# Gate products of FFN tile pairs by seven block products in place of eight

## The reference, cut to what matters

```
for l in range(2):                       # first block
    mod = silu(c) @ w_ada[l] + b_ada[l]  # nine vectors of 1024
    x = x + 0.5 * g1 * swiglu(modulate(x, sh1, sc1), ffn1_gate[l], ffn1_up[l], ffn1_down[l])
    x = x + g2 * token_mix(modulate(x, sh2, sc2), ...)
    x = x + 0.5 * g3 * swiglu(modulate(x, sh3, sc3), ffn2_gate[l], ffn2_up[l], ffn2_down[l])
x = rms_norm(x) * final_norm
# second block
x = x + merged @ w_o
h2 = rms_norm_2(x, norm2_g)
x = x + square(relu(h2 @ w_up)) @ w_down

def modulate(x, shift, scale): return rms_norm(x) * (1 + scale) + shift
def swiglu(u, w_gate, w_up, w_down): return (silu(u @ w_gate) * (u @ w_up)) @ w_down
```

## Time and profile before

| | us |
|---|---|
| median of three runs | 3475.17 (3474.67 to 3475.22) |
| the profiled execution | 3478.61 |
| its span | 3476.8 |
| PE busy | 3429.5 (99%) |
| weight loads, DVE, ACT busy | 2745.0, 1755.9, 1194.8 |

### The profile page before, as it was taken

How to read it: one execution, slowest core, us unless ns; L and a number is a source line. 1 busy time by engine, 2 the same in 40 slices (tenths; PEclk the granted TensorE clock), 3 DMA queues, 4 the chain that set the end, 5 groups by cost and what they waited for, 6 DMA issues and landing times.

```text
span 3476.8 us, 40836 instructions
## 1 busy us (share of the span) xinstructions
PE 3429.5 (99%) x16684; PEld 2745.0 (79%) x16684; DVE 1755.9 (51%) x3020; ACT 1194.8 (34%) x2015; POOL 263.1 (8%) x220
## 2 busy tenths in 40 slices
PE   9999999999999999999999999999999999999999
PEld 7888786778888788887777888887778777878887
DVE  7666446565666733334655643334453555364433
ACT  3222236543222322223555332223322344233322
POOL 0000210002000200021100100013011000020000
PEclk9999999999999999999999999999999999999999
DMA  7565321123565533223210322322222223122332
GB/s 252 201 215 187 107 89 63 43 70 118 190 220 194 183 99 101 93 95 107 72 49 25 109 91 81 111 82 93 75 80 72 68 70 120 40 94 91 98 102 79
DMA packets 120361, 376.36 MB, mean 108 GB/s; under 512 B 13296, under 2 KB 28272, under 8 KB 120176
## 3 DMA queue, kind: packets, MB, share of 16 engines
q1 hardware_dynamic: 120176, 373.76, 32.7%
...
## 4 chain that ended last, share of the span: by engine, by line
PE 93%; DVE 4%; ACT 2%; issue 0%; DMA 0%; POOL 0%; SPq 0%; DVEq 0%; ACTq 0%; POOLq 0%
PE ps L449 27%; PE ps L451 26%; PE ps L450 26%; PE ps L671 2%; PE ps L694 2%; PE ps L566 2%; PE ps L483 1%; PE ps L484 1%; PE ps L485 1%; PE ps L499 1%; PE ps L492 1%; DVE s_wl L1481 1%; ACT s_wh L964 0%; PE ps L536 0%; PE ps L538 0%
## 5 line engine op out<-in xcount | busy, mean ns | idle before, releaser
L1481 DVE TENSOR_TENSOR s_wl<-s_raw,s_wh 128x1024 fp32r<-128x1024 f32 (+3 forms) x645 | 706.1, 1096 | 899.5 <-ACT s_wh L964 898.3
L449 PE MATMUL ps<-s_uh,s_wh 128*128 128x512 f32 x2824 | 1129.3, 400 | 12.4 <-DVE s_ul L1542 3.8
L451 PE MATMUL ps<-s_ul,s_wh 128*128 128x512 f32 x2824 | 1105.6, 392 | 0.5 <-issue 0.5
L450 PE MATMUL ps<-s_uh,s_wl 128*128 128x512 f32 x2824 | 1105.3, 391 | 0.0
L964 ACT ACTIVATE s_wh<-s_raw 128x1024 fp32r<-128x1024 f32 (+3 forms) x645 | 588.0, 913 | 731.0 <-PE ps L451 536.3
L449 PEld LDWEIGHTS ps<-s_uh,s_wh 128*128 128x128 f32 x2824 | 533.6, 189 | 156.2 <-issue 42.1
L451 PEld LDWEIGHTS ps<-s_ul,s_wh 128*128 128x128 f32 x2824 | 533.1, 189 | 114.3 <-issue 0.9
L450 PEld LDWEIGHTS ps<-s_uh,s_wl 128*128 128x128 f32 x2824 | 533.4, 189 | 107.9 <-issue 2.2
L451 PE MATMUL ps<-s_fl,s_wh 128*128 128x512 f32 x960 | 378.2, 394 | 0.0
L449 PE MATMUL ps<-s_fh,s_wh 128*128 128x512 f32 x960 | 378.2, 394 | 0.0
L450 PE MATMUL ps<-s_fh,s_wl 128*128 128x512 f32 x960 | 378.2, 394 | 0.0
...
## 6 DMA issues: line engine op xcount, KB each, us to landing
...
```

The costliest lines, as they stand in the source:

```text
L449: TE.matmul(o, w_hi(i, k), h, start=first, stop=False)
L450: TE.matmul(o, w_lo(i, k), h, start=False, stop=False)
L451: return TE.matmul(o, w_hi(i, k), l, start=False, stop=last)
L1481: V.tensor_tensor(wl[w][:, 0:n], raw[t % NRAW][:, 0:n], wh[w][:, 0:n].bitcast(F32), SUB).then_inc(*s_lo.up(("lo", t)))
```

## The change

For every second gate tile from some tile of the stage on (`by_seven`), two neighbouring tiles, that is 256 output columns, are made together, 42 such pairs in all: 7 in f10, 9 each in f20, f11 and f21, 8 in up. Two row blocks by two column blocks of weights against two halves of the tokens are a product of 2x2 by 2x2 blocks, which takes eight block products; here it takes seven, of 256 token columns each, over four pairs of row blocks (`seven`). Eight of 512 columns over eight row blocks are 48 matmuls for the two tiles; seven by three by four are 84 of 256 columns. This asks for:

- sums of weights: DVE makes three more 128x128 weight blocks of each tile and changes one, in four instructions, before ACT rounds it (`get`); the tile then has 896 columns where a plain one has 1024, and there are four of them for two plain ones;
- mixtures of activations: ACT keeps u in float32 in uu, a second write beside uh; DVE makes four blocks of 128x256 for each pair of row blocks (`mixture`), ACT rounds them (th), DVE takes the rest (tl), once per stage and pair of row blocks, at plain tiles ahead of the first pair by seven (`mixture_of`);
- a combination of the seven products from four banks, by one ACT and four DVE instructions (`first_product`, `combine`); then silu or relu on both tiles at once in the buffer quad, and multiplication and splitting from there.

Chunks of 11 hidden tiles become rounds of 12 and then 10. The modulation tiles are placed anew: 56 in f10 as before; 48 in f20, none beside its plain tiles; 24 in f11, in its down phases. Some waits are put at other places for it.

```diff
-CHUNK_FF = 11
+ROUND = 12
...
+def rounds(nf):
+    return [(0, ROUND)] + [(a, min(10, nf - a)) for a in range(ROUND, nf, 10)]
+def by_seven(u, first, j):
+    if j < (8 if first else 4 if u else 6) or j % 2:
+        return False
+    return bool(u) or (j % 4 == 2 if j < ROUND else (j - ROUND) % 10 % 4 == 0)
+def mixture_of(u, first, j):
+    return {j_: kp for kp, j_ in enumerate((4, 5, 6, 7) if first else (0, 1, 2, 3) if u else (0, 2, 3, 4))}.get(j)
+def modulated_by(g, where, j):
+    return g == "g10" or g == "g20" and (where == "pair" or where == "seven" and j < ROUND)
+SEVEN = ((0, 3, 0), (2, 0, 0), (5, 0, 1), (4, 1, 0), (1, 1, 1), (6, 2, 0), (3, 2, 1))
...
+                if by_seven(u, ahead, j):
+                    t.extend((g, 2 * kp, 2, j * 128, 256, "seven") for kp in range(4))
+                    if side and modulated_by(g, "seven", j):
+                        t.append(side.pop(0))
+                    if u:
+                        fm(u, 8, j, modulated_by(g, "pair", j))
...
-    ADA = {"f10": [("ada0", g, k) for g in range(2, 9) for k in range(8)], "f20": [("ada1", g, k) for g in range(9) for k in range(8)]}
+    ADA = {"f10": [("ada0", g, k) for g in range(2, 9) for k in range(8)], "f20": [("ada1", g, k) for g in range(6) for k in range(8)],
+           "f11": [("ada1", g, k) for g in range(6, 9) for k in range(8)]}
...
+        def seven(g, name, c, banks, st):
+            o = [take((g, q), b) for q, b in enumerate(banks)]
+            for kp in range(4):
+                i = get(name, 2 * kp, c * 128)
+                pe.wait_ge(*s_dve["t", st, kp])
+                k1, k2 = 2 * kp, 2 * kp + 1
+                right = [(uh[:, k1, 0:256], ul[:, k1, 0:256]), (uh[:, k2, 0:256], ul[:, k2, 0:256])]
+                right += [(th[:, kp, j, :], tl[:, kp, j, :]) for j in (1, 0, 2)]
+                right += [(uh[:, k2, 256:512], ul[:, k2, 256:512]), (th[:, kp, 3, :], tl[:, kp, 3, :])]
+                for n, ((unit, q, half), (h, l)) in enumerate(zip(SEVEN, right)):
+                    out = o[q][:, 256 * half:256 * half + 256]
+                    w = slice(128 * unit, 128 * unit + 128)
+                    TE.matmul(out, wh[slot[i]][:, w], h, start=kp == 0 and half == 0, stop=False)
+                    TE.matmul(out, wl[slot[i]][:, w], h, start=False, stop=False)
+                    ins = TE.matmul(out, wh[slot[i]][:, w], l, start=False, stop=kp == 3 and (half == 1 or q == 3))
+                    if kp == 3 and n in (0, 2):
+                        ins.then_inc(*s_pe.up(("ps", (g, "second" if n else "first"))))
+                ins.then_inc(*s_pe.up(("w", i), *([("ps", (g, "all"))] if kp == 3 else [])))
+            if modulated_by(name, "seven", c):
+                side()
...
-                    n = todo[t][2] * todo[t][4]
-                    act.wait_ge(*landed(t))
+                    n = 896 if todo[t][5] == "seven" else todo[t][2] * todo[t][4]
+                    act.wait_ge(*(s_dve["weights", t] if todo[t][5] == "seven" else landed(t)))
...
+                if st in stages:
+                    if shift is None:
+                        SC.activation(uu(k), tmp[k % 4][:], ACT.Copy).then_inc(*s_act.up(("uu", st, k)))
+                    else:
+                        SC.activation(uu(k), tmp[k % 4][:], ACT.Identity, bias=shift(k), scale=1.0).then_inc(*s_act.up(("uu", st, k)))
...
+            def first_product(jj, free):
+                act.wait_ge(*s_pe["ps", (("g", st, jj), "first")])
+                act.wait_ge(*s_dve[free])
+                SC.activation(quad[0][:, 3, :], bank((("g", st, jj), 3))[:, 0:256], ACT.Copy).then_inc(*s_act.up(("P1", ("g", st, jj)), frees=(("g", st, jj), 3)))
+            def gate_of(jj):
+                act.wait_ge(*s_dve["C", ("g", st, jj)])
+                SC.activation(quad[0][:, 0:4, :], quad[0][:, 0:4, :], ACT.Silu if u else ACT.Relu).then_inc(*s_act.up(("gate", st, jj), ("gate", st, jj + 1)))
+            def hidden(jj, a0, src, tiles_=1):
+                act.wait_ge(*s_dve["prod", st, jj])
+                if a0:
+                    act.wait_ge(*s_pe["ps", ("d", st, earlier[a0], 7)])
+                j = jj - a0
+                SC.activation(fh[:, j:j + tiles_, :], src, ACT.Copy).then_inc(*s_act.up(*(("hh", st, jj + n_) for n_ in range(tiles_))))
...
+                    kp = mixture_of(u, first, jj)
+                    if kp is not None:
+                        act.wait_ge(*s_dve["T", st, kp])
+                        SC.activation(th[:, kp, :, :], quad[kp % 2][:, 0:4, :], ACT.Copy).then_inc(*s_act.up(("th", st, kp)))
...
+            while added[0] <= min(i + ahead + 1, len(todo) - 1):
+                t = added[0]
+                added[0] += 1
+                if todo[t][5] == "seven":
+                    w = lambda n: raw[t % NRAW][:, 128 * n:128 * n + 128]
+                    dve.wait_ge(*landed(t))
+                    V.tensor_tensor(w(4), w(1), w(3), ADD).then_inc(*s_dve.up(("S1", t)))
+                    dve.wait_ge(*s_dve.now())
+                    V.tensor_tensor(w(5), w(4), w(0), SUB).then_inc(*s_dve.up(("S2", t)))
+                    V.tensor_tensor(w(1), w(0), w(1), SUB).then_inc(*s_dve.up(("S3", t)))
+                    dve.wait_ge(*s_dve["S2", t])
+                    V.tensor_tensor(w(6), w(2), w(5), SUB).then_inc(*s_dve.up(("weights", t)))
...
+            def combine(jj):
+                g_, q = ("g", st, jj), quad[0]
+                two_ = lambda b: bank((g_, b))[:].rearrange("p (a n) -> p a n", a=2)
+                dve.wait_ge(*s_pe["ps", (g_, "second")])
+                dve.wait_ge(*s_act["P1", g_])
+                V.tensor_tensor(q[:, 0:5:4, :], q[:, 3:4, :].broadcast_to([128, 2, 256]), two_(0), ADD).then_inc(*s_dve.up(("C1", g_), frees=(g_, 0)))
+                dve.wait_ge(*s_pe["ps", (g_, "all")])
+                dve.wait_ge(*s_dve.now())
+                V.tensor_tensor(q[:, 1:3, :], q[:, 4:5, :].broadcast_to([128, 2, 256]), two_(1), ADD).then_inc(*s_dve.up(("C2", g_)))
+                dve.wait_ge(*s_dve.now())
+                V.tensor_tensor(q[:, 3, :], q[:, 2, :], bank((g_, 1))[:, 0:256], ADD).then_inc(*s_dve.up(("C3", g_), frees=(g_, 1)))
+                dve.wait_ge(*s_dve.now())
+                V.tensor_tensor(q[:, 1:3, :], q[:, 1:3, :], two_(2), ADD).then_inc(*s_dve.up(("C", g_), frees=(g_, 2)))
+            def product(jj, at, up):
+                dve.wait_ge(*s_act["gate", st, jj])
+                if up:
+                    dve.wait_ge(*s_pe["ps", ("u", st, jj)])
+                    V.tensor_tensor(at, at, bank(("u", st, jj))[:], MUL).then_inc(*s_dve.up(("prod", st, jj), frees=("u", st, jj)))
+                else:
+                    V.tensor_tensor(at, at, at, MUL).then_inc(*s_dve.up(("prod", st, jj)))
+            def hidden(jj, a0, src, n_=1):
+                j = jj - a0
+                dve.wait_ge(*s_act["hh", st, jj])
+                V.tensor_tensor(fl[:, j:j + n_, :], src, fh[:, j:j + n_, :].bitcast(F32), SUB).then_inc(*s_dve.up(*(("h", st, jj + i) for i in range(n_))))
+            def mixture(kp):
+                q = quad[kp % 2]
+                k1, k2 = uu(2 * kp), uu(2 * kp + 1)
+                dve.wait_ge(*s_act["uu", st, 2 * kp + 1])
+                V.tensor_tensor(q[:, 0, :], k1[:, 256:512], k1[:, 0:256], SUB).then_inc(*s_dve.up(("T1", st, kp)))
+                dve.wait_ge(*s_dve.now())
+                V.tensor_tensor(q[:, 1, :], k2[:, 256:512], q[:, 0, :], SUB).then_inc(*s_dve.up(("T2", st, kp)))
+                dve.wait_ge(*s_dve.now())
+                V.tensor_tensor(q[:, 2, :], q[:, 1, :], k1[:, 0:256], SUB).then_inc(*s_dve.up(("T3", st, kp)))
+                V.tensor_tensor(q[:, 3, :], k2[:, 0:256], q[:, 1, :], SUB).then_inc(*s_dve.up(("T", st, kp)))
+            def mixture_rest(kp):
+                dve.wait_ge(*s_act["th", st, kp])
+                V.tensor_tensor(tl[:, kp, :, :], quad[kp % 2][:, 0:4, :], th[:, kp, :, :].bitcast(F32), SUB).then_inc(*s_dve.up(("t", st, kp)))
...
+                    kp = mixture_of(u, first, jj)
+                    if kp is not None:
+                        mixture(kp)
+                    if u and jj and not (first and jj < 4):
+                        fm(u, 8, jj, 0, st, modulated_by(g, "plain", jj))
+                    if kp is not None:
+                        mixture_rest(kp)
+                    product(jj, s[:], u)
+                    if not (u and by_seven(u, first, jj + 1)):
+                        hidden(jj, a0, s[:].unsqueeze(1))```

**Start of stage f20, ACT.** Below is what stands there behind the last rounding of u, before and then now. s_uu is the kept u, s_th the rounded mixtures, s_wh rounded weights, s_tmp the gate's output, s_fh the hidden tile.

```order
L964 ACTIVATE s_wh<-s_raw 128x1024
L1043 ACT_TABLE_LOAD
L1043 ACTIVATE s_tmp<-ps 128x512
L1049 ACTIVATE s_fh<-s_tmp 128x512
L964 ACTIVATE s_wh<-s_raw 128x1024
```

(40 more changed lines are left out.)

145 lines of the change are left out of this document (98 added, 47 removed).

## The result

| | median us | lowest to highest, runs |
|---|---|---|
| before | 3474.67 | 3470.46 to 3475.22, 5 |
| changed | 3485.89 | 3476.07 to 3493.00, 5 |

The account below looks back on a forecast made before the run. PE, busy for 99% of the span, was taken to bound the kernel; -20.2 + 10 + 7.8 + 10.5 + 6.0 + 2.1 = +16.2 us on 3475.2 gave 3491, range 3461 to 3508.

Parts of the forecast that it names:

- What PE saves: In pairs by seven: 10.40 us instead of 10.88, a gain of 0.48 a pair, 20.2 us for 42 pairs.
- the part on top: On PE, a matmul's time beyond its columns at 2.4 GHz: 13.4 ns on uh and ul, 20.0 on th and tl.
- the third rival: Pairs by seven: th and tl run like uh, gain 33, waits as forecast, +3, 3478 us; chance 0.10.
- The first rival: Matmuls on PE: time on top is a share of columns, a pair 9.68, gain 50, total 3461 us; chance 0.14.
- its sign, under 117 ns: On PE: starts of 256-column matmuls less than 117 ns apart would speak for the first rival.
- (a): f10, pairs 4 to 7: mixtures with two modulation tiles make 13.1 us a pair, PE needs 10.88; waits 10 us.
- (b): Starts of f20, f11 and f21: u1's weights 2.6 us late each, table load in the chain; 7.8 in all.
- (c): Start of up: mixtures and first sums make the tiles by seven late, PE waits 10.5 us.
- (d): Pairs by seven: DVE waits for ACT, 0.5 us a pair with three modulation tiles, 0.1 with two; 6.0 in all.
- (e): Small ones: two round ends in up 0.8 us each, 1.7; the write of uu about 0.4; 2.1 in all.
- The second: Rival: gain as forecast, half of (a), (b), (c), nothing for (d): +2 or a little less, 3474 us; chance 0.17.
- the fourth: Rival: DVE bounds every pair by seven, 1 us more for each of 42, (a) to (c) full, 3515; chance 0.08.

Follow-up runs that it names:

- The repeat: The changed kernel run again with no edit, for a second trace: 3476.83 us over 12 runs, ratio 1.0011 to the kernel before.

## Why the prediction came out as it did

**What PE saves** failed in its size: forecast 0.48 a pair and 20.2 us, measured 1.10 and 46.2. I had kept the part on top at the full 13.4 and 20.0 ns of the earlier trace rows because 280 columns had 12.2, and I gave th and tl the 20.0 because they lie where fh and fl lie. Measured are 11.6 and 10. The larger error is th, which runs no slower than uh, as the third rival had it: 48 x 42 matmuls by 0.010 are 20 of the missing 26 us. The Trainium skill (TensorE: Matmul & The Clock Gate, Back-to-back issue gap) states N / 2.4 + 2.5 ns for an isolated matmul, 109 for 256 columns; the runs have 116.4, so it does not give the spacing of this stream. The first rival, 9.68 a pair, named the size, with 9.78 measured, and its sign, under 117 ns, came. Its reason holds in part at most: by it uh and ul would keep 6.7 of the 13.4 on top, and they keep 11.6. Its total, 3461, did not come, since the waits were larger than forecast.

**(a)** right. Forecast: a period of 13.1 and 10 us; measured 12.76 and 9.2 up to and with the first pair by seven, and the experiment with one modulation tile fewer shows that it is the handing over between ACT and DVE, not DVE's load: DVE is busy for 114.7 of the phase's 141.8, 81%, where the prediction named nine tenths as a sign. **(b)** right in mechanism: forecast 2.6 late at three starts, measured 2.5 each (7.5 for 7.8), with the table load in the chain as forecast. No drain came with the load: silu starts 0.01 after it. What I had not priced is the clock: 1.5 each behind two of them. **(c)** right in mechanism, the size in part by luck: 10.5 forecast, all as waits, 11.4 measured, of it only 7.2 waits for weights and, behind them, two stretches of 3.4 at half clock, 3.0. **(d)** half right: 2.4 for the five pairs of f10's second round, 0.5 each as priced for three modulation tiles, and 2.0 for the four of f20's first; but f10's first gate phase lost 3.5 beside the 9.2 of (a), where its two pairs were priced at 1.0, and it was 2.4 as well for f20's second round, where pairs have two and I said 0.1. The 18 pairs of f11 and f21 lost nothing beyond the start, as said, those of up a little (e). **(e)** 4.2 instead of 2.1: both kinds of round end in up cost 1.4 where I said 0.8, and the two later gate phases lose 0.7 each.

Waits and clock 45.9 for 36.4, gain 46.2 for 20.2: the forecast's +16.2 should have been 0. The five runs' +10 lie between, and the profile's +11.5 is in the untouched second block (+14.6, against -3 in the rest). The repeat at 1.0011 fits the zero. So the number was near by luck, for a reason that the sum does not contain; the sign, slower, held in the first five runs and could not be told from no change in the next twelve.

Two of the rivals' sums do not follow from their own terms. The second, half of (a), (b) and (c) and nothing for (d), is -20.2 + 14.2 + 2.1 = -4, 3471 and not 3474; the fourth, 42 us more with (a) to (c) in full, is 3527 at least, not 3515. Neither changes the forecast.

What stays open: which executions get the half-clock stretch in the second block. Three of the four profiles with the changed kernel's f10 had 27 to 37 us in one piece, from 2968 to 2971 on; of the others the one without pairs by seven and with places for the modulation tiles had 17 us in that part, and the rest at most 7. PE's work ahead of it is the same in the two profiles shown. Nor are long executions the changed kernel's own: of the 29 runs of before beside the repeat five took 3482.7 to 3487.6, at a granted clock of 0.989 to 0.990 where most had 0.992. No run here separates the cause.
